# One-hots for the crossing of PEER gates: half of a batch's tokens move from VectorE to GpSimd, and the last gate store and the first rounding of products change places

## The chip, the cores and the metric

The kernel runs on one core of one Trainium2 chip. The metric is device time in microseconds, the median of several executions; lower is better. The engines are named as the profile names them: PE is TensorE (PEld its weight loads), DVE is VectorE, ACT is ScalarE, POOL is GpSimd, SP is the queue that issues the big loads. ACTq is ScalarE's queue when it issues a DMA.

## The reference

Three two-layer transformer blocks run one after the other on 256 tokens of 1024 channels, in float32. The change touches only `peer_ffn` of the third block, which runs twice. It picks 128 of 16384 experts for each token (8 heads, the best 16 of each) and mixes them by a softmax gate:

```python
top_s, top_i = lax.top_k(s_half, PEER_TOPK)
cand_s = top_s[..., 0, :, None] + top_s[..., 1, None, :]
cand_i = top_i[..., 0, :, None] * PEER_N_KEYS + top_i[..., 1, None, :]
best_s, best_pos = lax.top_k(cand_s.reshape(B, S, PEER_HEADS, n_cand), PEER_TOPK)
experts = jnp.take_along_axis(cand_i.reshape(B, S, PEER_HEADS, n_cand), best_pos, axis=-1)
gate = jax.nn.softmax(best_s, axis=-1)
...
h = jax.nn.gelu(jnp.einsum('ted,td->te', u[ec], xc))
return jnp.einsum('te,ted->td', gc.astype(h.dtype) * h, v[ec])
```

## The kernel before, in words

The kernel doesn't gather experts. It computes all 16384 hidden values of every token as dense products and multiplies them by a gate matrix that is zero except at the chosen experts. An expert is a pair of keys (first, second), so the gate matrix of one token is 128x128.

**Slabs.** All weights stream from HBM in slabs of 128x2048 float32 (1 MB). SP loads them into a ring of four. ACT rounds each to a high part (`round_slab`, L1367), DVE subtracts to get the low part (`rest_slab`, L1839), and PE multiplies in three passes per product (high x high, high x low, low x high: L626, L627, L628). Each engine goes through the slabs in program order. An "up" slab makes two 128-row groups of hidden values (e = 0 and e = 1, each called a half slab below, 24 matmuls), a "down" slab consumes two.

**The crossing.** Up slabs 32 to 45 of a PEER stage (HALF = 32, EXTRA = 14) are interleaved with the building of the gates. There are 32 batches of 8 tokens, spread over 24 of the 28 half slabs in the pattern 1, 1, 2. For one batch:

- DVE makes the one-hot rows of the first keys of all 8 tokens in one instruction (`one_hots`, L2479, 128x1024) and then the one-hot rows of the second keys times the gate, one instruction a token (L2482, 128x128, eight of them; the key and the gate of the slot are two per-partition scalars). It signals `hot`.
- PE waits for `hot` and multiplies the two for each token (`cross`, L1346) into one of three PSUM bank pairs (`v.crossings`), and signals `crossed`.
- DVE multiplies the lower half of the keys straight from PSUM onto the hidden values (`multiply`, L2497), then makes the one-hots of the batch after the next, into the buffer that `crossed` has freed. There are two buffers.
- ACT copies the upper half of the keys out of PSUM (`stage_gates`, L1765) and issues the store of the batch before to HBM (`store_gates`, L1772). There are two staging buffers, so the copy of a batch waits for the store of the batch two before. These gates come back later (`return_gates`).

DVE's program order in this stretch is: at every second half slab `rest_slab`; then for each batch `multiply(b)`, `one_hots(b+2)`.

**The end of the crossing.** After up slab 45, ACT stores the last batch's gates, waits for both store semaphores, and only then rounds the first gated hidden values (`separate`, L1809). DVE makes their low part (L2511), and PE starts the first down slab (`expert_down`), which writes the four banks of bank pairs 0 and 1.

POOL has no instruction in a PEER stage before the change.

Of the kernel before, what the change touches and what calls it, by code (L numbers as in the profile page):

```python
# [13 lines left out]
ALU = mybir.AluOpType  # L14
# [5 lines left out]
TT = T // P  # L20
# [17 lines left out]
NKEYS = 128  # L38
# [6 lines left out]
BATCH = 8  # L45
BATCHES = T // BATCH
# [114 lines left out]
class Machine:  # L161


    def __init__(self, nc, dram, out, ctx, plan):
# [95 lines left out]
        self.key_scored, self.key_shown, self.activated = signal("key_scored"), signal("key_shown"), signal("activated")  # L260
        self.gate_shifted, self.gate_powered, self.gate_ready = signal("gate_shifted"), signal("gate_powered"), signal("gate_ready")
        self.slots_turned, self.slotted = signal("slots_turned"), signal("slotted")
        self.hot, self.crossed, self.staged = signal("hot"), signal("crossed"), signal("gates_staged")
        self.gates_stored = [signal(f"gates_stored{i}", 16) for i in range(2)]
        self.gates_back = [signal(f"gates_back{i}", 16) for i in range(RETURNS)]
# [281 lines left out]
def peer_views(k):  # L547
    v = Views()

    v.hidden = k.carve(2 * HALF + 2 * EXTRA, T)  # L550
    end = k.taken
    k.taken = 0
    v.h = k.carve(DC, T)
    norm_views(k, v)
    k.taken = 2 * HALF * T
    v.keys, v.s, v.cand = k.carve(2 * PH, P), k.carve(PH, 4, P), k.carve(2, TT, 256)
    assert k.taken <= end
    k.taken = end
    v.slots = k.carve(3, T)
    mark = k.taken  # L560
    v.hot = k.carve(4 * TOPK, TOPK)
    k.taken = mark
    v.firsts = k.carve(2, BATCH, P)
    v.seconds = [k.carve(BATCH, NKEYS)]
    assert k.taken <= k.room_words - 4 * 2 * T
    k.taken = mark
    v.returned = k.carve(RETURNS, BATCH, NKEYS // 2)

    k.taken = k.room_words - 4 * 2 * T
    v.seconds.append(k.carve(BATCH, NKEYS))  # L570
    v.staged = k.carve(2, BATCH, NKEYS // 2)
    assert k.taken <= k.room_words
    v.crossings = [k.wide_banks[i].rearrange("p (t n) -> p t n", n=NKEYS) for i in (0, 1, 3)]

    k.taken = k.room_words - 4 * 2 * T
    v.chosen, v.q, v.at = k.carve(TT, 3, NSEL), k.carve(2, T), k.carve(2, TT, TOPK, dt=U32)
    v.best, v.found, v.index = k.carve(2, 4, TOPK), k.carve(2, 4, TOPK, dt=U32), k.carve(2, 4, TOPK)
    v.part, v.ranks, v.small = k.carve(4, TOPK, dt=U32), k.carve(4, TOPK), k.carve(TT, 3, PH)
    v.tops = [v.chosen[:, i, 2, :].rearrange("p (h j) -> p h j", h=PH) for i in range(TT)]

    v.seq = peer_order()
    v.up_at = [v.seq.index(("up", r)) for r in range(ROUNDS)]
    v.down_at = [v.seq.index(("down", r)) for r in range(ROUNDS)]

    late = HALF + EXTRA
    v.place = [2 * r if r < late else 2 * (r - late) for r in range(ROUNDS)]
    windows = 2 * EXTRA - 4
    v.batches = [range(BATCHES * (s - 2) // windows, BATCHES * (s - 1) // windows) if 2 <= s < 2 + windows else range(0) for s in range(2 * EXTRA)]
    return v
# [16 lines left out]
class TensorE:  # L606
# [716 lines left out]
    def expert_down(self, r, e):  # L1323
        k, nc = self.k, self.k.nc
        if e == 0:
            self.pair = self.take()
            nc.tensor.wait_ge(k.hidden_ready.sem, k.hidden_ready.at(r + 1))
        high, low = self.pair
        at = FIRST_HIDDEN + 2 * (r % 2) + e
        for c in range(DC):  # L1330
            cols = slice(e * D + c * P, e * D + (c + 1) * P)
            mm = self.product(k.banks[c // 2][:, (c % 2) * T:(c % 2 + 1) * T], (high[:, cols], low[:, cols]),
                              (k.hidden[:, at, 0, :], k.hidden[:, at, 1, :]),
                              r == 0 and e == 0 and c % 2 == 0, r == ROUNDS - 1 and e == 1, skip_group_check=True)
        if e == 1:
            mm.then_inc(k.slab_done.up())

    def cross(self, v, b):

        k, nc = self.k, self.k.nc  # L1340
        bank = v.crossings[b % 3]
        nc.tensor.wait_ge(k.hot.sem, k.hot.at(b + 1))
        if b >= 3:
            nc.tensor.wait_ge(k.staged.sem, k.staged.at(b - 2))
        for t in range(BATCH):
            mm = nc.tensor.matmul(bank[:, t, :], v.firsts[:, b % 2, t, :], v.seconds[b % 2][:, t, :], start=True, stop=True)  # L1346
        mm.then_inc(k.crossed.up())


class ScalarE:  # L1350
# [361 lines left out]
    def peer(self, v, l):  # L1712
        k, nc = self.k, self.k.nc
        self.stage_enters(True)
        self.normed_input_with_keys(v, l)
        for hd in range(PH):
            self.round_slab()
            if hd >= 1:
                self.show_keys(v, hd - 1)
            self.evacuate(hd, v.q, self.projected(hd, 0))  # L1720
        self.show_keys(v, PH - 1)
        for r in range(HALF):
            self.round_slab()
            self.activate(v, r)
        for r in range(HALF, HALF + EXTRA):
            self.round_slab()
            if r == HALF:
                for i in range(TT):
                    nc.scalar.wait_ge(k.gate_shifted.sem, k.gate_shifted.at(i + 1))
                    nc.scalar.activation(v.tops[i], v.tops[i], ACT.Exp).then_inc(k.gate_powered.up())  # L1730
            for b in v.batches[2 * (r - HALF)]:
                self.stage_gates(v, b)
            self.activate(v, r)
            if r == HALF:
                for i in range(TT):
                    nc.scalar.wait_ge(k.slots_turned.sem, k.slots_turned.at(i + 1))
                    nc.scalar.activation(v.slots[:, 0:3, i * P:(i + 1) * P], k.banks[6 + i][:, 0:3 * P].rearrange("p (a t) -> p a t", a=3),
                                         ACT.Copy).then_inc(k.slotted.up())
            for b in v.batches[2 * (r - HALF) + 1]:
                self.stage_gates(v, b)  # L1740
        self.store_gates(v, BATCHES - 1)
        for i in range(2):
            nc.scalar.wait_ge(k.gates_stored[i].sem, k.gates_stored[i].at(BATCHES // 2))
        self.separate(v, 0)
        for r in range(ROUNDS):
            if r + 1 < ROUNDS:
                self.separate(v, r + 1)
            self.round_slab()
            if r + HALF + EXTRA < ROUNDS:
                self.round_slab()  # L1750
                self.activate(v, r + HALF + EXTRA)
            if r < RETURN_LEAD:
                self.return_gates(v, r)
            for s in range(2 * (r - HALF + EXTRA), 2 * (r - HALF + EXTRA) + 2):
                for b in v.batches[s] if 0 <= s < 2 * EXTRA else ():
                    if b + RETURN_LEAD < BATCHES:
                        self.return_gates(v, b + RETURN_LEAD)

    def stage_gates(self, v, b):

        k, nc = self.k, self.k.nc
        nc.scalar.wait_ge(k.multiplied.sem, k.multiplied.at(b + 1))
        if b >= 2:
            nc.scalar.wait_ge(k.gates_stored[b % 2].sem, k.gates_stored[b % 2].at(b // 2))
        nc.scalar.activation(v.staged[:, b % 2], v.crossings[b % 3][:, :, NKEYS // 2:NKEYS], ACT.Copy).then_inc(k.staged.up())  # L1765
        if b >= 1:
            self.store_gates(v, b - 1)

    def store_gates(self, v, b):
        k, nc = self.k, self.k.nc  # L1770
# [45 lines left out]
class VectorE:  # L1816
# [655 lines left out]
    def one_hots(self, v, b):  # L2472

        k, nc = self.k, self.k.nc
        t0 = b * BATCH
        iota = k.const("iota")
        if b >= 2:
            nc.vector.wait_ge(k.crossed.sem, k.crossed.at(b - 1))
        nc.vector.tensor_tensor(v.firsts[:, b % 2], v.slots[:, 0, t0:t0 + BATCH].unsqueeze(2).to_broadcast([P, BATCH, P]),  # L2479
                                iota.unsqueeze(1).to_broadcast([P, BATCH, P]), ALU.is_equal)  # L2480
        for t in range(BATCH):
            hot = nc.vector.tensor_scalar(v.seconds[b % 2][:, t, :], iota, v.slots[:, 1, t0 + t:t0 + t + 1], v.slots[:, 2, t0 + t:t0 + t + 1],  # L2482
                                          ALU.is_equal, ALU.mult)
        hot.then_inc(k.hot.up())
# [30 lines left out]
class GpSimd:  # L2515
# [95 lines left out]
    def fox(self, v):  # L2611
        self.stage_enters(False)
        self.add_squares(v)


class SyncE:
    def __init__(self, k):
# [16 lines left out]
def program(nc, dram, out, ctx, stages):  # L2634
# [11 lines left out]
    for stage, *args in stages:  # L2646
# [37 lines left out]
        if stage == "peer":  # L2684
            v = peer_views(k)
            pe.peer(v)
            act.peer(v, args[0])
            dve.peer(v, args[0])
        if stage == "fox":
            v = fox_views(k)  # L2690
            pe.fox(v)
            act.fox(v)
            dve.fox(v)
            pool.fox(v)
# [178 lines left out]
```

## Time and profile before

| quantity | value |
|---|---|
| median of 3 executions | 4419.83 us (4419.68 to 4426.2) |
| the profiled execution, its own time | 4424.73 us |
| its span | 4423.4 us |
| mean granted TensorE clock | 0.967 of full speed |
| PE busy | 4125.6 us, 93% of the span |
| DVE busy | 2885.4 us, 65% |
| ACT busy | 1957.4 us, 44% |
| POOL busy | 184.6 us, 4% |
| HBM traffic | 161 GB/s over the span |
| crossing of the first PEER stage | about 2728 to 2884 us |
| crossing of the second PEER stage | about 3773 to 3928 us |

Times inside the profile are microseconds from the start of the span. The profiled execution is 4.9 us (0.1%) above the median. A granted clock of 1.00 means TensorE's upper level (2.4 GHz), 0.50 its lower (1.2 GHz).

### The profile page before, as it was taken

Reading aid. Unit: us, or ns where it says so; the run is one execution under the profiler, and the core shown is the slowest. Engines: PE = TensorE matmul, PEld = TensorE weight load, DVE = VectorE, ACT = ScalarE, POOL = GpSimd, SP = SyncE. Lnnn points to the kernel's source line nnn. Section 1 sums busy time; section 2 is a strip of 40 time slices with the busy share of each in tenths; the row PEclk is TensorE's granted clock in tenths of the full one; section 3 lists DMA queues with packets and bytes.
Section 4 is the critical chain, followed back from the end, with each engine's and each line's share of the span. In section 5 each row is a group of like instructions: output and inputs, shape, how many; then the busy total and the mean of one; then the engine's idle time right before and its main releaser. Section 6 shows DMA issues by size and latency. Waiting matters only on the chain.

```text
span 4423.4 us, 70553 instructions
## 1 busy us (share of the span) xinstructions
PE 4125.6 (93%) x29950; PEld 3797.9 (86%) x29950; DVE 2885.4 (65%) x4317; ACT 1957.4 (44%) x2492; POOL 184.6 (4%) x219
## 2 busy tenths in 40 slices
PE   7989999899997999979988899899999899889998
PEld 6878888788786888868887899899998799889998
DVE  6666676666754767557645699944855589964664
ACT  4445454454543545445425444334444444334443
POOL 0011000110000000011012000000000000000000
PEclk9989999899999999989988999999999999999999
DMA  5523545245454454423541354445754345345653
GB/s 197 189 102 134 189 173 190 102 143 190 160 184 127 166 187 178 164 87 143 186 152 62 111 182 163 142 172 186 252 193 142 115 172 182 136 157 184 237 201 143
DMA packets 118602, 716.08 MB, mean 162 GB/s; under 512 B 13952, under 2 KB 19728, under 8 KB 37008
## 3 DMA queue, kind: packets, MB, share of 16 engines
q1 hardware_dynamic: 90864, 660.64, 42.1%
q10 hardware_dynamic: 26400, 43.28, 2.8%
q0 software_dynamic: 1024, 7.64, 0.4%
q8 instruction: 238, 3.90, 0.4%
q14 instruction: 76, 0.62, 0.0%
HBM read 690.38 MB, written 21.13 MB: 161 GB/s over the span
## 4 chain that ended last, share of the span: by engine, by line
PE 74%; DVE 15%; ACT 5%; DMA 2%; issue 2%; POOL 1%; ACTq 1%; POOLq 0%; DVEq 0%; SPq 0%
PE psum L697 21%; PE psum L626 13%; PE psum L628 12%; PE psum L627 12%; PE psum L698 10%; DVE slab_low L1839 4%; ACT slab_high L1367 2%; DVE room L2482 2%; DVE room L2479 1%; DMA peer_gates<-room 1%; DVE x L1961 1%; POOL room L2535 1%; DVE room L2503 1%; PE psum L1044 1%; DVE room L2497 1%
## 5 line engine op out<-in xcount | busy, mean ns | idle before, releaser
L1839 DVE TENSOR_TENSOR slab_low<-slab,slab_high 128x2048 fp32r<-128x2048 f32 x622 | 1427.4, 2295 | 848.4 <-ACT slab_high L1367 845.9
L1367 ACT ACTIVATE slab_high<-slab 128x2048 fp32r<-128x2048 f32 x630 | 1186.4, 1883 | 522.5 <-PE psum L698 262.0
L697 PE MATMUL psum<-h_parts,slab_high 128*128 128x512 f32 x2816 | 998.6, 399 | 43.3 <-DVE h_parts L2147 39.7
L626 PE MATMUL psum<-h_parts,slab_high 128*128 128x256 f32 x3136 | 922.6, 294 | 49.1 <-DVE h_parts L2147 21.7
L627 PE MATMUL psum<-h_parts,slab_high 128*128 128x256 f32 x3136 | 903.7, 288 | 0.0
L628 PE MATMUL psum<-h_parts,slab_low 128*128 128x256 f32 x3136 | 902.7, 288 | 0.0
L698 PE MATMUL psum<-h_parts,slab_low 128*128 128x256 f32 x2816 | 790.4, 281 | 0.0
L626 PE MATMUL psum<-hidden_parts,slab_high 128*128 128x256 f32 x2368 | 668.9, 282 | 27.9 <-DVE hidden_parts L2511 15.6
L697 PEld LDWEIGHTS psum<-h_parts,slab_high 128*128 128x128 f32 x2816 | 532.7, 189 | 177.6 <-issue 33.0
L626 PEld LDWEIGHTS psum<-h_parts,slab_high 128*128 128x128 f32 x3136 | 619.2, 197 | 66.5 <-issue 52.4
L628 PE MATMUL psum<-hidden_parts,slab_low 128*128 128x256 f32 x2368 | 663.0, 280 | 0.0
L627 PE MATMUL psum<-hidden_parts,slab_high 128*128 128x256 f32 x2368 | 662.6, 280 | 0.0
L627 PEld LDWEIGHTS psum<-h_parts,slab_high 128*128 128x128 f32 x3136 | 619.0, 197 | 2.5 <-issue 2.4
L628 PEld LDWEIGHTS psum<-h_parts,slab_low 128*128 128x128 f32 x3136 | 617.9, 197 | 0.0
L698 PEld LDWEIGHTS psum<-h_parts,slab_low 128*128 128x128 f32 x2816 | 535.2, 190 | 0.2
L697 PE MATMUL psum<-hidden_parts,slab_high 128*128 128x512 f32 x1408 | 495.5, 395 | 0.0
L626 PEld LDWEIGHTS psum<-hidden_parts,slab_high 128*128 128x128 f32 x2368 | 448.1, 189 | 37.9 <-issue 33.2
L628 PEld LDWEIGHTS psum<-hidden_parts,slab_low 128*128 128x128 f32 x2368 | 448.5, 189 | 0.0
L627 PEld LDWEIGHTS psum<-hidden_parts,slab_high 128*128 128x128 f32 x2368 | 448.1, 189 | 0.0
L698 PE MATMUL psum<-hidden_parts,slab_low 128*128 128x256 f32 x1408 | 396.1, 281 | 0.0
L697 PEld LDWEIGHTS psum<-hidden_parts,slab_high 128*128 128x128 f32 x1408 | 264.7, 188 | 63.0
L1449 ACT ACTIVATE room<-psum 128x512 f32<-128x512 f32 x176 | 104.8, 596 | 366.3 <-PE psum L698 366.3
(320 smaller groups left out, 4132.5 us busy)
## 6 DMA issues: line engine op xcount, KB each, us to landing
slab<-in_up SPq DMA_DIRECT2D x176, 1024.0 KB, 4.8
slab<-in_keys_up SPq DMA_DIRECT2D x128, 1024.0 KB, 4.8
slab<-in_keys_down SPq DMA_DIRECT2D x128, 1024.0 KB, 4.8
slab<-in_down SPq DMA_DIRECT2D x88, 1024.0 KB, 4.8
slab<-in_w_in SPq DMA_DIRECT2D x16, 1024.0 KB, 4.8
slab<-in_wq SPq DMA_DIRECT2D x16, 1024.0 KB, 4.8
peer_gates<-room ACTq DMA_DIRECT2D x64, 256.0 KB, 2.1
room<-peer_gates ACTq DMA_DIRECT2D x64, 256.0 KB, 4.9
```

Source lines behind the costliest of these rows:

```text
L626: nc.tensor.matmul(out, lhs[0], rhs[0], start=first, stop=False, **options)
L627: nc.tensor.matmul(out, lhs[0], rhs[1], start=False, stop=False, **options)
L628: return nc.tensor.matmul(out, lhs[1], rhs[0], start=False, stop=last, **options)
L697: nc.tensor.matmul(out, lhs[0], rhs, start=first, stop=False, **options)
L698: return nc.tensor.matmul(out[:, 0, :], lhs[1], rhs[:, 0, :], start=False, stop=last, **options)
L1044: mm = nc.tensor.matmul(k.banks[6][:, at:at + P], v.probs[:, n % 5, e, kt * P:(kt + 1) * P], v.diagonals[:, n % 3, e, :], start=True, stop ...
L1367: nc.scalar.activation(k.high[m % PARTS][:, 0:width], k.slabs[m % RING][:, 0:width], ACT.Copy).then_inc(k.rounded.up())
L1449: nc.scalar.activation(v.seconds[:, f % 2], k.bank_pairs[(f + k.first_pair) % 4][:, :, T:2 * T], ACT.Copy).then_inc(k.up_copied.up())
L1839: nc.vector.tensor_tensor(k.low[m % RING][:, 0:width], k.slabs[m % RING][:, 0:width], k.high[m % PARTS][:, 0:width], ALU.subtract).then_in ...
L1961: add = nc.vector.scalar_tensor_tensor(out=both, in0=k.bank_pairs[j][:, :, a * T:(a + 1) * T], scalar=0.5, in1=both, op0=ALU.mult, op1=ALU ...
L2479: nc.vector.tensor_tensor(v.firsts[:, b % 2], v.slots[:, 0, t0:t0 + BATCH].unsqueeze(2).to_broadcast([P, BATCH, P]), iota.unsqueeze(1).to_ ...
L2482: hot = nc.vector.tensor_scalar(v.seconds[b % 2][:, t, :], iota, v.slots[:, 1, t0 + t:t0 + t + 1], v.slots[:, 2, t0 + t:t0 + t + 1], ALU.i ...
```

## The change

Four of the eight second-key one-hots of a batch are made by POOL, in a new function `peer`, under its own semaphore `pool_hot`, for which PE also waits. The other four stay on DVE. The three PSUM bank pairs of the crossing are used in another order, so that the last batch doesn't lie in a pair that the down slabs write. The last batch's store is issued right behind its copy. ACT rounds the first hidden values before it waits for the stores, and PE's first down slab waits for the last staging copy instead.

```diff
@@ peer_views
-    v.crossings = [k.wide_banks[i].rearrange("p (t n) -> p t n", n=NKEYS) for i in (0, 1, 3)]
+    v.crossings = [k.wide_banks[i].rearrange("p (t n) -> p t n", n=NKEYS) for i in (1, 3, 0)]
@@ TensorE.expert_down
             self.pair = self.take()
+            if r == 0:
+                nc.tensor.wait_ge(k.staged.sem, k.staged.at(BATCHES))
             nc.tensor.wait_ge(k.hidden_ready.sem, k.hidden_ready.at(r + 1))
@@ TensorE.cross
         nc.tensor.wait_ge(k.hot.sem, k.hot.at(b + 1))
+        nc.tensor.wait_ge(k.pool_hot.sem, k.pool_hot.at(b + 1))
@@ ScalarE.peer
-        self.store_gates(v, BATCHES - 1)
+        self.separate(v, 0)
         for i in range(2):
             nc.scalar.wait_ge(k.gates_stored[i].sem, k.gates_stored[i].at(BATCHES // 2))
-        self.separate(v, 0)
@@ ScalarE.stage_gates
         if b >= 1:
             self.store_gates(v, b - 1)
+        if b == BATCHES - 1:
+            self.store_gates(v, b)
@@ VectorE.one_hots
-        for t in range(BATCH):
+        for t in range(BATCH // 2):
             hot = nc.vector.tensor_scalar(v.seconds[b % 2][:, t, :], iota, v.slots[:, 1, t0 + t:t0 + t + 1], v.slots[:, 2, t0 + t:t0 + t + 1],
                                           ALU.is_equal, ALU.mult)
@@ GpSimd
+    def peer(self, v):
+
+        k, nc = self.k, self.k.nc
+        self.stage_enters(True)
+        nc.gpsimd.wait_ge(k.slotted.sem, k.slotted.at(TT))
+        for b in range(BATCHES):
+            if b >= 2:
+                nc.gpsimd.wait_ge(k.crossed.sem, k.crossed.at(b - 1))
+            for t in range(BATCH // 2, BATCH):
+                at = b * BATCH + t
+                hot = nc.gpsimd.tensor_scalar(v.seconds[b % 2][:, t, :], k.const("iota"), v.slots[:, 1, at:at + 1], v.slots[:, 2, at:at + 1],
+                                              ALU.is_equal, ALU.mult)
+            hot.then_inc(k.pool_hot.up())
```

On ACT, at the end of a crossing, the order before is as follows (`peer_gates<-room` is the store, `hidden_parts<-room` the rounding of hidden values, `slab_high` the rounding of a slab).

```order
L1765 ACTIVATE room<-psum 128x512 [waits gates_stored1,multiplied]
L1772 DMA peer_gates<-room 128x512 [waits gates_staged]
L1367 ACTIVATE slab_high_58<-slab_50 128x2048 [waits slab_done,slab_arrived1]
L1800 ACTIVATE room<-psum 128x512 [waits slab_done]
L1772 DMA peer_gates<-room 128x512 [waits gates_staged]
L1809 ACTIVATE hidden_parts<-room 128x2x256 [waits multiplied,gates_stored1,gates_stored0]
L1809 ACTIVATE hidden_parts<-room 128x2x256 [waits multiplied]
```

After the change the same place reads as follows (line numbers are higher by 3 to 5).

```order
L1768 ACTIVATE room<-psum 128x512 [waits gates_stored1,multiplied]
L1777 DMA peer_gates<-room 128x512 [waits gates_staged] x2
L1371 ACTIVATE slab_high_58<-slab_50 128x2048 [waits slab_done,slab_arrived1]
L1805 ACTIVATE room<-psum 128x512 [waits slab_done]
L1814 ACTIVATE hidden_parts<-room 128x2x256 [waits multiplied]
L1814 ACTIVATE hidden_parts<-room 128x2x256 [waits multiplied,gates_stored1,gates_stored0]
```

The last store has moved ahead of a slab's rounding and of the activation that waits for PE, and the wait for stores stands in front of the second rounding of hidden values, not the first.

On POOL the new rows of a stage begin as follows; the stage had none.

```order
L2630 TENSOR_SCALAR room<-consts,room 128x128 [waits slotted,pool_move,x_done]
L2630 TENSOR_SCALAR room<-consts,room 128x128 x7
L2630 TENSOR_SCALAR room<-consts,room 128x128 [waits crossed]
L2630 TENSOR_SCALAR room<-consts,room 128x128 x3
L2630 TENSOR_SCALAR room<-consts,room 128x128 [waits crossed]
```

Four instructions follow each release by `crossed`, 128 in a stage. DVE's rows keep their order, with `x4` where `x8` stood behind each 128x1024 row.

## Rows read from the trace of the kernel before

**Rows 1.** The page: the span, and busy time of the engines.

```profile
span 4423.4 us, 70553 instructions
PE 4125.6 (93%) x29950; PEld 3797.9 (86%) x29950; DVE 2885.4 (65%) x4317; ACT 1957.4 (44%) x2492; POOL 184.6 (4%) x219
```

**Rows 2.** Busy time by stretch: PE, PEld, DVE, ACT, POOL; granted clock; DMA share, GB/s.

```profile
2740.00:2884.00 144.00, 122.71 (x1006) 120.17 (x1004) 138.98 (x313) 44.31 (x54) 0.00 (x0) 0.98 0.40 139
```

**Rows 3.** Groups of PE, first and second crossing: busy, mean ns | idle before, releaser.

```profile
L1346 PE MATMUL psum<-room 128*128 128x128 f32 x480 | 61.3, 282 | 21.3 <-DVE room L2482 21.3
L1346 PE MATMUL psum<-room 128*128 128x128 f32 x484 | 61.5, 281 | 20.3 <-DVE room L2482 20.3
```

**Rows 4.** The chain that ended last, in the first crossing: start us, us, what.

```profile
2762.98 0.60 DVE room L2497
2763.58 1.13 DVE room L2479
2764.71 2.05 DVE room L2482 x8
...
2774.34 2.20 DVE slab_low L1839
...
2777.18 5.56 DMA peer_gates<-room
```

**Rows 5.** Timeline of DVE: first and last gate multiply of each crossing.

```profile
2739.58 0.68 DVE L2497 TENSOR_TENSOR room<-psum,room 128x512 f32<-128x512 f32 x1
...
2883.49 0.69 DVE L2497 TENSOR_TENSOR room<-psum,room 128x512 f32<-128x512 f32 x1 [1.54 <-PE psum L1346]
...
3784.11 0.68 DVE L2497 TENSOR_TENSOR room<-psum,room 128x512 f32<-128x512 f32 x1
...
3927.03 0.69 DVE L2497 TENSOR_TENSOR room<-psum,room 128x512 f32<-128x512 f32 x1 [1.54 <-PE psum L1346]
```

**Rows 6.** Timeline of PE: a half slab, a crossing, the next half slab.

```profile
2755.07 0.36 PE L626 MATMUL psum<-h_parts,slab_high 128*128 128x256 f32 x1
...
2758.03 1.95 PE L1346 MATMUL psum<-room 128*128 128x128 f32 x16
2759.74 0.36 PE L626 MATMUL psum<-h_parts,slab_high 128*128 128x256 f32 x1
```

**Rows 7.** Groups of DVE by shape: a tensor_scalar with one scalar, SBUF to SBUF.

```profile
L2205 DVE TENSOR_SCALAR room<-room 128x256 f32<-128x256 f32 x16 | 4.9, 351 | 0.3
L2205 DVE TENSOR_SCALAR room<-room 128x128 f32<-128x128 f32 x16 | 3.9, 285 | 0.3
```

**Rows 8.** Timelines of POOL and DVE where both read SBUF; L2215's durations (ns).

```profile
395.50 4.69 POOL L2535 TENSOR_TENSOR room<-room 128x512 f32<-128x512 f32 x2
396.78 2.29 DVE L1839 TENSOR_TENSOR slab_low<-slab,slab_high 128x2048 fp32r<-128x2048 f32 x1 [3.40 <-ACT slab_high L1367]
...
867.26 1.19 POOL L2571 TENSOR_SCALAR room<-consts,room 128x128 f32<-128x128 f32 x2 [2.43 <-DVE room L2197]
867.41 0.49 DVE L2215 TENSOR_TENSOR hidden_parts<-room,hidden_parts 128x256 fp32r<-128x256 f32 x1 [0.25 <-ACT hidden_parts L1601]
...
L2215 DVE TENSOR_TENSOR hidden_parts<-room,hidden_parts x32: 403/420/489, 319.6 to 3504.5; 128x256 fp32r<-128x256 f32 x32
```

**Rows 9.** Timelines of ACT and PE at the first crossing's end.

```profile
2889.24 0.60 ACT L1800 ACTIVATE room<-psum 128x512 f32<-128x512 f32 x1 [2.51 <-PE psum L628]
2889.24 0.35 ACTq L1772 DMA_DIRECT2D peer_gates<-room  x1
2895.07 1.15 ACT L1809 ACTIVATE hidden_parts<-room 128x512 fp32r<-128x512 f32 x2 [5.24 <-DMA peer_gates<-room]
...
2896.57 0.55 PE L626 MATMUL psum<-hidden_parts,slab_high 128*128 128x256 f32 x1 [7.37 <-DVE hidden_parts L2511]
```

**Rows 10.** Busy time by stretch at the ends of both crossings, columns as in rows 2.

```profile
2892.00:2902.00 10.00, 5.43 (x25) 5.46 (x26) 3.58 (x3) 2.95 (x3) 0.00 (x0) 0.50 0.23 95
3936.00:3943.00 7.00, 2.85 (x13) 2.88 (x14) 2.66 (x3) 2.95 (x3) 0.00 (x0) 0.53 0.28 111
```

More of the change, by code:

```diff
@@ L262, in __init__ @@
         self.slots_turned, self.slotted = signal("slots_turned"), signal("slotted")
+        self.pool_hot = signal("pool_hot")
         self.hot, self.crossed, self.staged = signal("hot"), signal("crossed"), signal("gates_staged")
@@ L2688, in program @@
             dve.peer(v, args[0])
+            pool.peer(v)
         if stage == "fox":
```

## The prediction

> **What bounds the kernel now.** I read the page first. PE is busy 93% of the span and POOL 4% [rows 1]: an edit can only pay where PE waits. So I went to the two crossings, by stretch. In the first, 2740 to 2884, PE is busy 122.7 of 144 us, DVE 139.0, POOL nothing [rows 2]. The groups of PE say who it waits for: 21.3 us of idle time before L1346 in the first crossing and 20.3 in the second, all released by DVE's L2482, the one-hots that the change touches [rows 3].
>
> The chain of waits shows DVE's round for one batch: multiply 0.60, first one-hots 1.13, eight second one-hots 2.05, together 3.78 us. Every second half slab adds a subtraction of 2.20 [rows 4]. From the first multiply to the last is 143.9 us in the first crossing and 142.9 in the second [rows 5]. Checked against the steps: 31 rounds x 3.78 + 11 subtractions x 2.20 = 141.4, the rest are short waits. DVE is the pace maker.
>
> The second place is the end of a crossing: PE stands 7.37 us before the first down slab. ACT waits 5.24 us for a store that was issued at 2889.24, behind an activation that itself waited for PE, and rounds hidden values only at 2895.07 [rows 9]. The granted clock is 0.50 from 2892 to 2902, and 0.53 in the like place of the second stage [rows 10].
>
> **The change part by part: PE's floor.** PE needs 2.96 us for a half slab and 1.71 for a crossing behind it [rows 6]; where it waited, a crossing costs nearer 1.8, so I take 1.75. Between first and last multiply stand 23 half slabs and 31 crossings: 68.1 + 54.3 = 122.4 us, which agrees with the 122.7 busy. So the crossing can't give more than 21.5 and 20.5 us.
>
> **DVE's round after.** Four one-hots fewer take 1.03 off: 2.75 us. 31 x 2.75 + 11 x 2.20 = 109.5, below PE's floor, if POOL doesn't disturb it.
>
> **POOL's round.** The price of one new instruction, p, isn't in the trace: no POOL instruction there has two scalars and two operations. The nearest row is L2571, the same engine, shape and kind with one scalar and one operation: two take 1.19, that is 0.58 to 0.61 each [rows 8]. Below: 0.58, since the new one does all that this does. Above: a second operation as dear as the whole first, 1.2. I take 0.62, near the like row.
>
> DVE and POOL disturb each other. In [rows 8] two POOL instructions take 4.69 us around a DVE subtraction of 2.29: they stood still for most of it. The other way round is milder: a DVE instruction with two SBUF inputs that began 0.15 us into a POOL instruction took 0.49 where the median is 0.42. So a short POOL instruction uses the common path for a small part of its time. I price a DVE instruction that POOL meets at its length less 0.2 us: the first one-hots 0.93, a subtraction 2.0. For the four short DVE one-hots I take 0.27 together. Bounds: 0 if they don't disturb POOL, 1.03 if they stop it altogether. They might, because a tensor_scalar from SBUF to SBUF takes 285 ns for 128 elements and 351 for 256 [rows 7]: 0.52 ns an element, two for each that the 1.13 us for 1024 elements implies, so it may use both paths.
>
> POOL's chain between first and last multiply is then 31 x (4p + 0.93 + 0.27) + 11 x 2.0 = 59.2 + 124p. With p = 0.62 that is 136.1, above PE's 122.4 and DVE's 109.5, even if each of the four POOL instructions held DVE up by 0.16 (129). **So GpSimd becomes the pace maker**, with 143.9 - 136.1 = 7.8 us won in the first crossing and 6.8 in the second: 14.6 together. 0.01 us in p is worth 2.5 us of kernel time, and at p = 0.68 the crossings win nothing.
>
> The Trainium skill (SBUF — State Buffer, Who interferes with whom) says that the pair of ports which DVE and GpSimd share is an exclusive lock, held for the whole instruction by whichever came first, and that a DVE instruction with two SBUF inputs or in a two-port mode contends for it. By the 4.69 us the trace agrees for a DVE holder; by the 0.49 us it doesn't for a short GpSimd holder. What the rule gives if taken whole is the last rival below.
>
> **The stores.** ACT copies a batch only when the store of two before has landed, and one such store took 5.56 us on the chain [rows 4], beside a slab load, I take it. A slab's time in the crossing is at least 2 x 2.96 + 2.67 x 1.75 = 10.6 us and has one load, so about one store in 2.67 is that slow and I cost this at nothing; cover is the third PSUM pair. If it broke, a late copy would hold `slab_high`, then DVE's subtraction, then the multiply.
>
> **The end.** In the new order `separate(0)` follows the activation of 2889.24. ACT starts two such instructions some 0.5 apart, so it rounds at 2889.75, and PE starts 1.50 later as it did (2895.07 to 2896.57): 2891.25, not 2896.57 [rows 9]. That is 5.3 us a stage, 10.6 for both. The last store is now issued before the last up slab's activation and has some 5 us of cover (a slab's rounding and half a slab of PE); uncovered, it would delay the second rounding only, behind a down slab of 5.8 us. PE's new wait for the last copy costs nothing: ACT has made it before it reaches the activation. The clock: PE was busy 5.4 us of the half-speed 10 and 2.9 of the 7 [rows 10], of which half each, 2.7 and 1.4, is lost. With a stand of 2 us and not 7 I expect most of it back: 3.3, bounds 0 and 4.1. The bank order alone costs nothing; same banks, same copies.
>
> **Sum.** 14.6 + 10.6 + 3.3 = 28.5 us off the profiled execution, 4424.7 to 4396.2. This execution lies 4.9 above the median of the runs, so 4419.8 - 28.5 = 4391.3; I say 4390.
>
> **The rivals.**
>
> *Forecast* (p 0.58 to 0.67, GpSimd paces the crossing): 4381 to 4404. Chance 0.42.
>
> *PE paces the crossing.* POOL's meetings with DVE are fewer than priced, since POOL may be done before the subtraction. Then 21.5 + 20.5 + 13.9 = 56, so 4364. For: POOL starts a batch at `crossed`, at the same time as the multiply, which reads PSUM. Against: DVE's first one-hots start 0.60 later, inside POOL's 2.5. Chance 0.14.
>
> *The crossing gives nothing, only the end does.* p of 0.67 to 0.77: 124p takes back what DVE gave. At 0.68 the time is 4406, at 0.77 about 4428. For: one more scalar and one more operation in software. Against: nothing in the trace. Chance 0.26, of which 0.11 lies below 4411.
>
> *Slower.* The one mechanism is that POOL's instruction is dear: from p = 0.736 on the crossings lose the 13.9 of the end again, at 0.80 the time is 2 x 158.4 - 286.8 = 30.0 worse in the crossings, 16 in all, 4436; at 1.0 it is 4486. Every batch then waits for `pool_hot`, while DVE stands idle. Chance 0.13.
>
> *The path is held for POOL's whole instruction.* Then DVE's 1.13 + 1.03 and POOL's 4 x 0.58 of a batch can't overlap: 31 x 4.48 + 11 x 2.20 = 163.1, 19.7 a crossing worse, 39.4 - 13.9 = 25.5 slower, 4445. This is the skill's rule of the SBUF page. Against it stands the 0.49 us. Chance 0.05.
>
> **The numbers.** A measurement of this kernel tells 0.2%, 8.8 us, from no change. Below 4411 lie 0.42 + 0.14 + 0.11 = 0.67; between 4411 and 4428.6 lie 0.15; above, 0.18. The range of eight in ten runs from 4363, PE's floor, to 4430, which cuts off most of the slower cases. The forecast's own range is 4381 to 4404.
>
> **What the next profile would show.** L2630's undisturbed instructions at 0.62 us, its mean near 1.1 (the 1.20 a batch of meetings and 22 us of subtractions are recorded inside them), so POOL busy some 140 us more in each PEER stage. PE's idle time before L1350 put down to POOL and not to DVE, about 13 us in each crossing; near nothing if PE paces, over 21 if slower. First to last multiply 136 us. DVE's 128x1024 rows still near 1.21, and its short one-hots above 335 ns if POOL gets in between. PE's stand before the first down slab 2.0 us, granted clock 1.00 there. I am wrong if POOL's undisturbed instruction is far from 0.62, if the gaps of POOL behind subtractions are shorter than 2.0, or if the stores come to end ACT's waits in most batches.

## The result and the profile after

The changed kernel takes 4432.93 us, the median of 20 runs (4417.1 to 4447.65); the kernel before took 4421.41 beside it, the median of 20 (4406.32 to 4433.67). The ratio is 1.0025, with a 95% interval of 1.0014 to 1.0036: 11 us slower, between 6 and 16. The forecast was 4390, faster, range 4363 to 4430. Below, one of eight executions of the kernel with GpSimd's part alone took 8348.37 us, nearly twice the others, and is in none of the figures.

The page of the changed kernel, the engines, against [rows 1]:

```profile
PE 4127.6 (93%) x29950; PEld 3800.4 (86%) x29950; DVE 2825.6 (64%) x4061; ACT 1959.5 (44%) x2492; POOL 498.4 (11%) x475
```

This one execution took 4425.98 us, near the low edge of the runs; in experiment 6 another profile gives the same time and a third one 10 us more. DVE lost 256 instructions and 59.8 us (the step on DVE's round had 64 x 1.03 = 66). POOL gained the same 256 and 313.8 us, 157 in each PEER stage, where the forecast had some 140. So the first thing to look up is what one costs.

One source line of the changed kernel each (ns min/median/max, first and last start): POOL's new one-hots, DVE's remaining ones, DVE's first one-hots, and DVE's gate multiply.

```profile
L2630 POOL TENSOR_SCALAR room<-consts,room x256: 783/864/4725, 2723.9 to 3932.3; 128x128 f32<-128x128 f32 x128
L2487 DVE TENSOR_SCALAR room<-consts,room x256: 332/342/424, 2724.8 to 3930.7; 128x128 f32<-128x128 f32 x128
L2484 DVE TENSOR_TENSOR room<-room,consts x64: 1207/1216/1258, 2723.7 to 3928.7; 128x1024 f32<-128x1024 f32 x64
L2502 DVE TENSOR_TENSOR room<-psum,room x64: 677/691/694, 2737.2 to 3935.3; 128x512 f32<-128x512 f32 x64
```

The minimum of the first line is the price for which the forecast took 0.62: 0.783 us. DVE's own lines stand nearly where they stood (medians before: 335, 1209 and 679 ns); nothing there is held up for long. GpSimd's are: 1.22 on the mean in this stretch of POOL's timeline (ten batches of four), 4.89 a batch with the subtractions in it, and 12.50 for the first eight.

```profile
2723.88 12.50 POOL L2630 TENSOR_SCALAR room<-consts,room 128x128 f32<-128x128 f32 x8 [272.74 <-ACT room L1741]
...
2741.86 48.89 POOL L2630 TENSOR_SCALAR room<-consts,room 128x128 f32<-128x128 f32 x40 [0.45 <-PE psum L1350]
```

PE sees those first eight. Its timeline, at the first crossing's start:

```profile
2733.42 3.68 PE L1350 MATMUL psum<-room 128*128 128x128 f32 x16 [7.63 <-POOL room L2630]
```

And the first and the last gate multiply of each crossing, against [rows 5]:

```profile
2737.21 0.69 DVE L2502 TENSOR_TENSOR room<-psum,room 128x512 f32<-128x512 f32 x1 [4.60 <-PE psum L1350]
...
2886.47 0.69 DVE L2502 TENSOR_TENSOR room<-psum,room 128x512 f32<-128x512 f32 x1 [2.48 <-PE psum L1350]
...
3785.04 0.69 DVE L2502 TENSOR_TENSOR room<-psum,room 128x512 f32<-128x512 f32 x1 [4.58 <-PE psum L1350]
```

The last one, 3935.3, is in the line of L2502 above. First to last is 149.3 and 150.2 us where it was 143.9 and 142.9, and the first comes later too. Of the 64 multiplies 36 now wait for PE, 72.2 us in all, where two waited 3.1 us before. For what does PE wait? The view of L1350, idle time before it by releaser:

```profile
  issue: 81.5, 37
  DVE room L2487: 19.6, 16
  POOL room L2630: 15.1, 2
```

This view counts each wait twice, before the weight load and before the matmul. The matmuls alone waited 55.8 us: 15.1 at the two starts, 21.4 in the first crossing and 19.3 in the second (before: 21.3 and 20.3). "issue" means that the profile shows no releaser, and the name L2487 is not to be trusted either, so I went by the ends of the one-hots. In the first crossing all 13 waits of the matmuls end 0.10 us behind the end of GpSimd's last one-hot of the batch, when DVE's share had been done for 2.1 to 5.9 us. In the second crossing 11 of 12 do, and one, of 0.37 us, ends behind DVE's. An example from the crossing's end: POOL's last two begin at 2882.75 and take 1.56 us, to 2884.31, and PE's sixteen products start at 2884.41.

```profile
2882.75 1.56 POOL L2630 TENSOR_SCALAR room<-consts,room 128x128 f32<-128x128 f32 x2
...
2884.41 2.02 PE L1350 MATMUL psum<-room 128*128 128x128 f32 x16 [1.16 <-issue]
```

The end of the crossing went as planned. ACT and PE, timelines of the first one, against [rows 9]:

```profile
2892.22 0.60 ACT L1805 ACTIVATE room<-psum 128x512 f32<-128x512 f32 x1 [1.18 <-PE psum L629]
2892.71 1.14 ACT L1814 ACTIVATE hidden_parts<-room 128x512 fp32r<-128x512 f32 x2
...
2894.20 0.36 PE L627 MATMUL psum<-hidden_parts,slab_high 128*128 128x256 f32 x1 [2.02 <-DVE hidden_parts L2516]
```

The rounding starts 0.49 us behind the activation and PE stands 2.02 us, not 7.37.

By stretch (columns as in [rows 2]), the half-speed clock of [rows 10] has gone from the ends, but a new stretch of it stands at the starts, where PE waits for the first eight (the second line):

```profile
2889.00:2899.00 10.00, 7.98 (x69) 7.80 (x68) 5.88 (x4) 5.36 (x5) 0.00 (x0) 1.00 0.39 132
...
2729.00:2737.00 8.00, 3.58 (x17) 3.61 (x18) 3.62 (x2) 0.00 (x0) 7.37 (x6) 0.57 0.00 0
```

### The profile page after: what moved, and what is told of

It reads as the page before. It is cut to its first block, busy times and chain, and to the rows that moved or that the text cites. A ratio compares the mean times of both kernels' runs of the same rounds, so it can differ in the third digit from the quotient of the medians.

```text
span 4424.7 us, 70561 instructions
## 1 busy us (share of the span) xinstructions
PE 4127.6 (93%) x29950; PEld 3800.4 (86%) x29950; DVE 2825.6 (64%) x4061; ACT 1959.5 (44%) x2492; POOL 498.4 (11%) x475
## 4 chain that ended last, share of the span: by engine, by line
PE 79%; DVE 11%; ACT 5%; issue 2%; POOL 2%; DMA 1%; ACTq 1%; POOLq 0%; DVEq 0%; SPq 0%
PE psum L698 20%; PE psum L627 13%; PE psum L628 13%; PE psum L629 13%; PE psum L699 10%; DVE slab_low L1844 3%; ACT slab_high L1371 2%; PE psum L1350 2%; PE psum L1045 1%; DVE x L1966 1%; POOL room L2540 1%; DVE room L2508 1%; PE psum L1028 1%; DVE h_parts L2152 1%; PE psum L1058 1%
## 5 line engine op out<-in xcount | busy, mean ns | idle before, releaser
L2630 POOL TENSOR_SCALAR room<-consts,room 128x128 f32<-128x128 f32 x256 | 314.4, 1241 | 682.6 <-ACT room L1741 675.2
```

What stands on the lines that cost most here:

```text
L2630: hot = nc.gpsimd.tensor_scalar(v.seconds[b % 2][:, t, :], k.const("iota"), v.slots[:, 1, at:at + 1], v.slots[:, 2, at:at + 1], ALU.is_equ ...
```

## The experiments

Two theories stood at first. **A**: GpSimd's instruction is simply dearer than taken, so it paces the crossing and loses more than the end wins. **B**: the end or the new waits cost something that the milestones hide. Later came **C**: GpSimd-paced crossings vary between executions. All diffs are against the changed kernel where nothing else is said. "Crossing" is first to last gate multiply, first stage / second stage; "start" is the first multiply behind the first one-hots.

**1. Each half alone.** First the end without GpSimd's part (the edit in short):

```diff
 cross:  - wait pool_hot >= b + 1
 gates:  - for t in range(BATCH // 2):
         + for t in range(BATCH):
 GpSimd: - pool.peer(v)
```

> Only the edits of the end: the last store at its copy, the first rounding ahead of the wait for stores, the bank order. GpSimd has no part in it. Theory A (each part of the change has its own price, and they add up): PE's stand before the first down slab falls from 7.4 to 2.0 us in both stages, 10.6 us, and the half-speed stretches there go, 4.1 us: 14.7 us faster than before, ratio 0.9967. Rival B (the stand is given back later, since the slabs behind it are paced by loads): the profile shows the stand gone but the time is within 5 us of before.

Measured: 4410.38 against 4424.96, ratio 0.9972 [0.9959, 0.9986]. Crossing 144.4/141.1, PE's stand at the end 2.02/2.41 (before 7.37/7.42).

Then the kernel before, with GpSimd's part alone (the same three places the other way round):

> Only the one-hots of half the tokens on GpSimd, the end as before. Theory A: in the profile after the change, first to last multiply is 149.3 and 150.2 us and was 143.9 and 142.9, and the first multiply stands 2.7 us later behind the first one-hots: 2.7 + 5.4 and 2.7 + 7.3, so 18 us slower than before, ratio 1.004, GpSimd's undisturbed instruction 0.785 us. Rival C (the profiled execution was a lucky one and the crossings usually cost more, which is why the median of the whole change is 11 us above and its profile only 3): 25 us slower or more, ratio 1.006.

Measured: 4443.02, the median of seven executions, against 4424.96, ratio 1.0042 [1.0025, 1.0058]. Crossing 153.8/149.4, start 13.6/13.3. So the two halves have opposite signs (by the ratios 12.4 us faster and 18.6 slower), and add up to the whole within their intervals. B falls for the end's edits; the loss is all in GpSimd's part. The wait for `pool_hot` belongs to that part, but the memset kernel of experiment 2 keeps the wait and takes 4364.06 us, so it isn't the wait as such.

**2. What the instruction is made of.** Three kernels change only what GpSimd computes. One scalar and one operation:

```diff
-  v.slots[:, 1, at:at + 1], v.slots[:, 2, at:at + 1], ALU.is_equal, ALU.mult
+  v.slots[:, 1, at:at + 1], None, ALU.is_equal
```

> The whole change, but GpSimd's instruction has one scalar and one operation: it compares and leaves the gate out, so the gates of half the tokens are 1. Theory A, first form (the second scalar and the second operation cost the 0.2 us between 0.58 and 0.775): undisturbed instructions last 0.605 us, start to start 0.58, and first to last multiply falls by 31 x 4 x 0.195 = 24 us, down to PE's floor or DVE's round, 126 us. Second form (a comparison is dear by itself): the instruction stays near 0.785 and the crossing near 150.

Two operations, the second with a constant (`0.5` in place of `v.slots[:, 2, at:at + 1]`):

> The whole change; GpSimd's instruction keeps two operations but its second operand is the constant 0.5 and not a scalar from SBUF, so the gates of half the tokens are 0.5. One operation and one scalar gave 0.597 us undisturbed, two of each 0.785. If the second operation costs the difference, about 0.78; if the fetch of the second scalar does, about 0.60; shares of both lie between.

No input at all, `nc.gpsimd.memset(v.seconds[b % 2][:, t, :], 0.0)`:

> The whole change, but GpSimd writes zeros (memset) in place of its one-hots: it reads nothing from SBUF, and the gates of half the tokens are left out. If DVE's instructions with two SBUF inputs (the first one-hots, the subtraction) stop GpSimd through the common read path alone, no memset is longer than its undisturbed 0.2 to 0.3 us. If they take the path both ways, memsets of 1 to 2.5 us appear, as with the one-hots (1.74 and 2.69 us against 0.79).

GpSimd's line in each of the three, in this order:

```profile
L2630 POOL TENSOR_SCALAR room<-consts,room x256: 592/600/2743, 2725.9 to 3900.6; 128x128 f32<-128x128 f32 x128
```
```profile
L2630 POOL TENSOR_SCALAR room<-consts,room x256: 710/762/4681, 2726.6 to 3917.9; 128x128 f32<-128x128 f32 x128
```
```profile
L2630 POOL MEMSET room<- x256: 199/204/312, 2720.0 to 3864.6; 128x128 f32 x128
```

The minima are the undisturbed ones: 0.592 with one scalar and one operation (the 0.58 to 0.61 of [rows 8]), 0.710 with a second operation, 0.783 with a second scalar on top. So a second operation costs 0.12 us and a second scalar 0.07; the forecast had 0.02 for both together. The times were 4396.7, 4413.21 and 4364.06 in one execution each, with crossings of 133.4/137.6, 141.5/147.9 and 128.1/128.6. The first missed what was expected (126). In its first crossing GpSimd stood idle for 18.7 us, so GpSimd alone didn't pace it; ACT waited 18.0 us for stores there and 33.6 in the second, and DVE 9.8 and 14.1 us for ACT's rounding of slabs. Experiment 3 takes this chain apart.

The maxima carry the other finding. The 198 memsets that met none of DVE's short one-hots took at most 0.207 us, 123 of them beside a subtraction or the first one-hots; the 58 that met a short one-hot took up to 0.312. The forms that read take up to 2.7 us (one scalar) and 4.7 us (the other two) beside DVE's subtractions. The timelines of the changed kernel show when a one-hot of GpSimd is stopped. Where DVE's first one-hots had begun before it, or began at most 0.20 us behind its start, it took 1.50 to 2.15 us (64 times, median 1.81); beside a subtraction under the same condition 2.47 to 4.73 (25 times, median 2.69). Where the DVE instruction began 0.23 us or more behind its start, it took 0.78 to 0.87 (59 times), as beside the short one-hots alone. What stops GpSimd is its own read beside DVE instructions with two inputs in SBUF. The Trainium skill says so (SBUF — State Buffer, Who interferes with whom): such a DVE instruction contends with a GpSimd instruction that reads SBUF and not with one that only writes. By that part of the rule, the traces agree.

**3. Fewer tokens for GpSimd.** Two of eight, a constant `POOL_TOKENS = 2` (the edit in short):

```diff
-        for t in range(BATCH // 2):
+        for t in range(BATCH - POOL_TOKENS):
-            for t in range(BATCH // 2, BATCH):
+            for t in range(BATCH - POOL_TOKENS, BATCH):
```

> The whole change with two tokens of eight on GpSimd and not four. Theory A (GpSimd's own instruction is too dear, 0.775 us from start to start, and four of them with their meetings are the round): GpSimd's round is now 2 x 0.775 + 1.05 for the first one-hots + 0.7 for its share of subtractions = 3.3 us, DVE's 3.26 + 0.78 = 4.04, PE's floor 3.95. First to last multiply 125 to 128 us in each crossing, so 2 x 17 + 14.7 less some 3 at the start = 45 us faster than before, ratio 0.990. Rival D (what hurts is that the two engines meet at all, not how many instructions GpSimd has): GpSimd is still stopped by every first one-hots and subtraction and PE waits for it as often; the crossing stays near 140 us and the whole gains under 20.

Measured: 4402.43 against 4424.96, ratio 0.9950 [0.9934, 0.9966], crossing 138.5/137.0. Faster, but half of what A said. The waits of 2748 to 2870 in this kernel (us in total, times, longest):

```profile
ACT room L1771 <- DMA peer_gates<-room: 26.4, 8, 5.8
...
DVE slab_low L1847 <- ACT slab_high L1374: 6.6, 4, 3.4
```

That is the chain which the forecast had named and costed at nothing: a staging copy waits for a store, `slab_high` comes late behind it on ACT, and DVE's subtraction waits up to 3.4 us. In the first crossing of the changed kernel the same wait of DVE is at most 0.3 us. In its second crossing it is not: there ACT waited four times for stores, 18.1 us, and DVE 12.3 us for `slab_high`, 3.9 at the longest. So the next kernel issues each store at its own copy:

```diff
-        if b >= 1:
-            self.store_gates(v, b - 1)
-        if b == BATCHES - 1:
-            self.store_gates(v, b)
+        self.store_gates(v, b)
```

> Two tokens of eight on GpSimd, the end edits, and now every store issued right behind its own copy, not at the copy of the next batch. In the run with two tokens alone, first to last multiply took 138.5 and 137.0 us, where DVE's own round (31 x 3.29 + 11 x 2.20 = 126 us) and PE's floor (122) are lower; the waits put 10 us of DVE's idle time down to late rounding of slabs on ACT, which stood 32 us waiting for stores. Theory A (the store, issued a batch late, holds ACT, which holds the slab's rounding, which holds DVE): a store has a batch more time, ACT hardly waits for one, the crossing falls to 126 to 130 us, and the whole is 40 us faster than before, ratio 0.991. Rival D (the meetings of DVE and GpSimd make the difference of 12 us): the crossing stays at 137 to 138 us and the ratio at 0.995.

Measured: 4384.28 against 4426.26, ratio 0.9915 [0.9891, 0.9939], crossing 131.2/131.2. The waits of the same stretch:

```profile
DVE slab_low L1844 <- ACT slab_high L1374: 3.6, 10, 0.4
```

ACT's wait for stores is down from 26.4 us to 1.7, and DVE's longest is 0.4. Two controls put the same store edit where the pace is slower: on the end alone and on the changed kernel with its four tokens.

> The end edits and every store at its own copy, nothing on GpSimd. Theory A: before, DVE lost only some 3 us a crossing behind ACT's waits for stores, since its own round (3.78 a batch) is slow; so 2 to 4 us a crossing faster than the end edits alone, ratio 0.996. Rival: ACT pays 0.6 us a batch for waiting on its own copy before it issues the store, and nothing or a loss comes out.

Measured: 4408.29 against 4426.26, ratio 0.9964 [0.9948, 0.9979], crossing 141.1/140.9: against the 0.9972 of the end alone no difference that can be told.

> The whole change, four tokens on GpSimd, and every store at its own copy. Theory A (with four tokens GpSimd paces, and ACT and its stores have time): no gain, first to last multiply 149 to 150 us as without. If the stores hold this version too, 3 us or more less.

Measured: 4429.88 in one execution (the kernel before took 4420.48 beside it), crossing 147.7/147.8. The changed kernel's six crossings in three profiles are 148.6 to 153.8, so this is 1 to 6 us shorter, and one profile can't tell whether the forecast of no gain or that of 3 us holds. With two tokens the store edit took 7.3 and 5.8 us off the crossings; with GpSimd's four or DVE's eight one-hots no gain in time is shown.

**4. The start.** Four tokens, but GpSimd begins with the third batch (DVE makes the first two alone):

```diff
+POOL_TOKENS = 4
+POOL_FROM = 2
-        nc.tensor.wait_ge(k.pool_hot.sem, k.pool_hot.at(b + 1))
+        if b >= POOL_FROM:
+            nc.tensor.wait_ge(k.pool_hot.sem, k.pool_hot.at(b + 1 - POOL_FROM))
-        for t in range(BATCH // 2):
+        for t in range(BATCH - (POOL_TOKENS if b >= POOL_FROM else 0)):
-        for b in range(BATCHES):
+        for b in range(POOL_FROM, BATCHES):
```

> The whole change with four tokens on GpSimd, but only from the third batch on; the first two batches' one-hots are all DVE's. Theory A (at the start GpSimd's eight instructions run against two first one-hots, eight second ones and two subtractions of DVE, 12.5 us for 6.2 of work, and PE waits 7.6 us for them): the first multiply goes back from 13.5 to 10.8 us behind the first one-hots, first to last multiply stays at 149 to 150. Rival: the loss only moves to the third batch and the last multiply stands at the same distance from the first one-hots, 163 us.

Measured: 4438.81 in one execution. The start is back at 10.9, and nothing is won: the crossing is 154.9/153.2, the last multiply 165.8/164.1 behind the first one-hots (changed kernel 162.8/163.7, and 167.3/162.1 in its second profile). The rival holds, and not Theory A. The first eight only moved; while GpSimd paces, its work has to be done some time.

**5. The best share.** Three tokens from the third batch on, the store edit, and the change's end:

> Three tokens of eight on GpSimd from the third batch on (the first two batches all on DVE), the end edits, every store at its copy. Theory A (the slower of two rounds sets the pace): DVE 3.02 a batch and 11 x 2.20 = 117.8 us, GpSimd 3 x 0.775 + 1.05 a batch and 11 x 1.9 = 125.5, PE 122.4. With two tokens the crossing took 131.2 us for a DVE round of 126, so GpSimd's 125.5 should give 129 to 131, the same as with two within a us or two, ratio 0.991. Rival D (each more GpSimd instruction costs by its meetings): 135 us or more.

Measured: 4383.44 against 4420.48, ratio 0.9914 [0.9896, 0.9933], crossing 126.8/126.6, start 10.9. The crossings are shorter than the 129 to 131 that were expected. This version beats both kernels, the one before by 0.86%. Its first crossing by stretch:

```profile
2733.00:2879.00 146.00, 134.35 (x1136) 132.21 (x1134) 133.49 (x246) 53.61 (x63) 121.10 (x90) 1.00 0.44 153
```

PE is busy 134 of 146 us, DVE 133, POOL 121, and the clock is 1.00: all three rounds are nearly equal. Between first and last multiply, 126.8 us, PE is busy 118.4. In time this kernel equals the one with two tokens: its 4.4 us a crossing, less 1.0 at each start, are within what the two intervals leave open.

**6. How steady a profile is.** Changed kernel twice more, kernel before once more:

> The changed kernel as it is, profiled once more. Its first profile accounts for 3 us of loss in the two PEER stages (from the first one-hots to the first down slab 170.5 and 171.4 us, before 167.7 and 166.8, less 4.3 that the first down slabs win by the clock), the medians differ by 11. Theory C (the crossing that GpSimd paces varies with the clock, since PE idles in it; the first profile had few half-speed stretches): 153 us or more from first to last multiply in one crossing or both, and more half-speed time than 34 us in the crossings. Rival E (the crossing is always 149 to 150, and the missing 8 us lie outside the PEER stages or in chance): 149 to 150 again.

> The changed kernel a third time, for the spread. As for the second: Theory C 149 to 155 us a crossing from run to run, Rival E 149 to 150.

> The kernel before, profiled once more as a control. Both theories: 143 to 144 us a crossing again, since DVE paces it and DVE has no clock that falls; Theory C asks that its crossings vary less than those after.

Measured: 4425.96, 4436.15 and 4420.32; one more execution of the kernel before took 4431.71 beside them. The table gives us a stage, first / second; "start" and "crossing" as above, "stand" is PE's idle time before the first down slab.

| kernel, profile | start | crossing | stand | first one-hots to first down slab |
|---|---|---|---|---|
| before | 10.8 / 10.8 | 143.9 / 142.9 | 7.4 / 7.4 | 167.7 / 166.8 |
| before again | 10.8 / 10.8 | 144.5 / 140.9 | 7.4 / 7.4 | 168.4 / 164.8 |
| changed | 13.5 / 13.5 | 149.3 / 150.2 | 2.0 / 2.0 | 170.5 / 171.4 |
| changed again | 13.6 / 13.5 | 153.7 / 148.6 | 2.0 / 2.0 | 175.0 / 169.8 |
| changed, third | 13.6 / 13.5 | 153.8 / 148.6 | 2.0 / 2.0 | 175.1 / 169.8 |

C holds in part. The first GpSimd-paced crossing is 149 us in one profile and 154 in two; the second is 149 to 150 in all three. The kernel before keeps within 0.6 us in the first stage and 2.0 in the second. The two crossings of the changed kernel's second profile, from first to last multiply, show what makes one longer:

```profile
2732.15:2885.85 153.70, 132.29 (x1050) 130.07 (x1050) 110.68 (x193) 45.51 (x54) 144.50 (x120) 0.94 0.38 134
```
```profile
3786.51:3935.10 148.59, 126.98 (x1050) 124.74 (x1050) 110.54 (x193) 45.52 (x54) 144.06 (x120) 0.98 0.38 139
```

PE does the same 1050 matmuls in both and is idle equally long (21.4 and 21.6 us), but is busy for 5.3 us more in the first, where the clock was 0.94. GpSimd is busy equally long, and waits 8.0 us for PE's products, not 3.3. So the lower clock makes the crossing longer: PE's own work takes longer and frees GpSimd's buffer later. A longer crossing that lowered the clock would have more idle time of PE in it. Why the clock was lower in one crossing than in the other stays open.

With means over the profiles and both stages together: start +5.5, crossings +15.3, stands -10.7, together +10.0 us to the first down slab. Behind that, in the first 12 us of down slabs, half-speed time was 8.8 and 7.2 us before and 0, 3.4 and 3.4 after; half of the difference, 2.9 us, is my estimate of what that gives back. That makes 7.1 us, inside the measured 6 to 16. The other 4 are within what the rest of the program varies by from one execution to the next (the first one-hots of the first stage began at 2718.6 to 2728.6 us in the three profiles of the changed kernel), and I can't place them.

## Why the prediction was wrong

**The step that failed is the price p.** I took p from the row of the same engine and shape with one scalar and one operation, and added 0.02 for one of each more. It was 0.783. My own formula, 59.2 + 124p, gives 156.3 with that where the forecast had 136.1, against a measured 149 to 154: the shape of the working was right, its one free number was not. The threshold was right as well: from p = 0.736 on I had the change slower, and it is. The rival "Slower" is what happened, at a chance of 0.13. Its own sum at 0.78 has the crossings 25 us worse and the end 14 better, 11 slower. That is the measured size, but not by its terms: the crossings lost only 15, and the start, which it left out, 5. Nothing excluded that rival: for it I wrote "one more scalar and one more operation", against it "nothing", and still took the low end.

**The rivals that didn't happen.** PE doesn't pace: its matmuls are idle before L1350 for 21.4 and 19.3 us in the crossings (I had 13 each, over 21 if slower), and wait for GpSimd. The path isn't held for GpSimd's whole instruction: L2487 takes 342 ns and L2484 1216, where held ones would have shown GpSimd's 783 on top. The crossings as a whole neither win nor break even.

**GpSimd as the pace maker: right**, shown by PE's starts at its ends (24 of 25 waits in the crossings), by experiment 3 (fewer tokens, shorter crossing) and by 4. **The meetings: right in size.** Per batch 4.89 us were seen in ten batches, with their share of subtractions; 4 x 0.783 leaves 1.76, where I had 1.20 and 11/31 of 2.0, that is 1.91. One by one: 1.02 us for a stop by the first one-hots (1.81 less 0.79; I had 0.93) and 1.91 by a subtraction (I had 2.0). The 0.2 us for which I let a short GpSimd instruction use the common path came out as well: it was stopped by what began up to 0.20 us behind its start and not by what began 0.23 us or more behind.

**PE's floor: 4 us too high.** I had 122.4; at a clock of 1.00 PE is busy for 118.4 of the 126.8 us of the version with three tokens. The 122.7 with which I had it agree was measured at a clock of 0.98.

**The start: not in the sum at all.** The count ran from first to last multiply. But GpSimd's first eight instructions meet two first one-hots, eight short ones and two subtractions before PE has anything: 12.50 us, 2.7 us more a stage until the first multiply. Experiment 4 suggests, in one profile, that this isn't a separate loss to be mended; it is the same shortage, paid early.

**The end: right.** 5.3 a stage were forecast, and 5.35 and 5.40 came (stand 7.37 to 2.02; 7.42 to 2.02). The end alone gave 12.4 us by its ratio (0.28% of 4424.96; the interval is 6 to 18), where the sum had 13.9 (10.6 + 3.3).

**The clock: right at the ends, left out at the starts.** I expected 1.00 at the ends, and it is in the first profile; the two others have one half-speed stretch of 3.4 us behind the first down slab. I gave no price to PE's long wait for GpSimd at the starts. From the first one-hots to the first multiply, both stages together, there was no half-speed time before and 14, 18 and 18 us after. Between first and last multiply the difference isn't clear: 14 and 27 us in the two profiles before, 21, 23 and 23 after, none in the two best versions. What such time costs is shown only for work: 13 us more of it in the first crossing of the changed kernel's second profile made PE busy for 5.3 us more.

**The stores: nearly right for this kernel, by luck of its pace.** I said what would be late if the cover broke. In one of the changed kernel's six crossings it broke (12.3 us of waits of DVE), and that crossing was 150.2 us where the same one took 148.6 in the other profiles; the clock was lower there too (0.95 against 0.98), and the 1.6 us can't be split between the two. With two tokens it does break: the crossing stays at 138 where it could be 131, and 16 us of the gain in time are lost (22 us by the ratio where 38 can be had).

## What to carry to other kernels

Work that is given to a slow helper is priced by an instruction with the same number of scalars and operations, or measured alone first: here 0.16 us in one instruction, 128 times a crossing, turned a gain into a loss. Share the work so that the rounds of helper and giver are equal and count what stops the helper. With the store edit, two and three of eight each won 38 us (three begun at the third batch), and four of eight was 9 us slower than the kernel before, in one execution. When one pace maker is relieved, go down the list of what is covered only because of it (here a store, a copy, a rounding) before the gain is booked.

## What the runs showed of the hardware

- GpSimd's tensor_scalar of 128x128 fp32, undisturbed: 0.592 us with one scalar and one operation, 0.710 with a second operation, 0.783 with a second scalar; DVE's same form with two takes 0.332. A memset of that size takes 0.199.
- A GpSimd instruction that reads is stopped by DVE instructions with two SBUF inputs: 0.78 us became 1.81 beside one of 1.21, 2.69 beside one of 2.29 (medians), and 4.7 beside two of the latter in a row. That holds where the DVE instruction had begun or began within 0.20 us; where it began 0.23 us or more behind GpSimd's start, GpSimd took at most 0.87. One that only writes isn't (at most 0.207 us beside the same two).
- DVE's short one-hots, with one SBUF input, lengthen GpSimd's instructions a little, whether they read (0.86 us for 0.78) or only write (0.28 at the median for 0.20, 0.312 at the most).
- DVE's short instructions hardly notice GpSimd: 342 ns at the median, where the kernel before has 335. A second profile of the kernel before, without GpSimd's work, has 408 at an unchanged pace, so differences of this size in a recorded duration say nothing.
- TensorE's granted clock falls where PE waits long for GpSimd: 0.57 from 2729 to 2737 us, with 7.63 us of idle time before the first products. In crossings with waits of at most 3.4 us there was 21 to 23 us of half speed in 300, no clear difference from DVE's pace (14 and 27), and none in the versions with two and three tokens and the store edit.
